# Low halves on VectorE alone, half splits one turn sooner, and RWKV's key factor on VectorE, in a two-block transformer kernel

## The reference

```python
z = u @ w_in[i]
a = jax.nn.sigmoid(a0 + xa @ a2)
kk = heads(k * k_k)
kk = kk / jnp.maximum(jnp.sqrt(jnp.sum(kk * kk, axis=-1, keepdims=True)), 1e-12)
k = k * (1.0 + (a - 1.0) * k_a)
...
h = h + rmsnorm(merged @ w_out[i], mix_post_norm[i])
f = rmsnorm(h, ffn_pre_norm[i])
f = jnp.square(jax.nn.relu(f @ w_ff_in[i])) @ w_ff_out[i]
h = h + rmsnorm(f, ffn_post_norm[i])
e = (p[i] @ w_ple[i]) * jax.nn.sigmoid(h @ w_ple_gate[i])
```

## Time and profile before

| what | us |
|---|---|
| median of 3 runs | 1006.86 (1006.79 to 1007.04) |
| the profiled execution | 1004.86 |
| its span, first to last instruction | 1003.0 |
| TensorE busy | 947.7 |
| VectorE, ScalarE, GpSimd busy | 567.2, 431.0, 222.5 |
| GpSimd: 33 halves, 54 steps of 384 columns, 4 halves of W_ple_gate | 86.6, 82.1, 11.6 |

### The profile page before, as it was taken

The page is one execution under the profiler, slowest core; times in us unless marked ns, Lnnn a source line. Parts: engine busy times, 40 slices in busy tenths (PEclk is TensorE's granted clock), DMA queues, the critical chain, the costliest instruction groups (busy, mean ns, idle before and its releaser), DMA issues.

```text
span 1003.0 us, 15853 instructions
## 1 busy us (share of the span) xinstructions
PE 947.7 (94%) x6780; PEld 776.2 (77%) x6780; DVE 567.2 (57%) x867; ACT 431.0 (43%) x687; POOL 222.5 (22%) x151
## 2 busy tenths in 40 slices
PE   6999999989989999999989999989999999999996
PEld 3988887767558988888769988766568688888875
DVE  1558665653474444677864656864663344444883
ACT  2575234343342334455542433663440345454560
POOL 1000000100000254566630450000000023434570
PEclk9999999999999999999999999999999999999998
DMA  9334333212534865555337673332465367665531
GB/s 335 101 126 143 110 89 125 85 45 85 210 132 160 249 194 181 197 191 187 125 126 169 153 213 116 126 126 85 160 218 147 89 166 198 178 192 186 190 104 42
DMA packets 134949, 151.85 MB, mean 151 GB/s; under 512 B 15936, under 2 KB 106304, under 8 KB 134752
## 3 DMA queue, kind: packets, MB, share of 16 engines
q1 hardware_dynamic: 133952, 147.14, 47.4%
q10 hardware_dynamic: 928, 3.70, 1.0%
HBM read 149.78 MB, written 1.05 MB: 150 GB/s over the span
## 4 chain that ended last, share of the span: by engine, by line
PE 79%; DVE 12%; ACT 5%; issue 2%; DMA 1%; POOL 0%; POOLq 0%; SPq 0%; ACTq 0%; DVEq 0%
PE psum L806 10%; PE psum L695 7%; PE psum L697 7%; PE psum L696 7%; PE psum L758 7%; PE psum L807 6%; PE psum L1292 4%; PE psum L778 3%; PE psum L779 3%; PE psum L787 3%; PE psum L701 2%; PE psum L864 2%; ACT parts L1697 2%; PE psum L854 2%; PE psum L855 2%
## 5 line engine op out<-in xcount | busy, mean ns | idle before, releaser
L1697 ACT ACTIVATE parts<-low 128x1024 fp32r<-128x1024 f32 (+2 forms) x234 | 238.6, 1047 | 110.6 <-PE psum L697 61.9
L695 PE MATMUL psum<-parts 128*128 128x512 f32 (+2 forms) x424 | 171.7, 405 | 11.6 <-DVE parts L2430 8.6
L2430 DVE TENSOR_TENSOR parts<-low,parts 128x1024 fp32r<-128x1024 f32 (+2 forms) x115 | 144.1, 1261 | 55.0 <-ACT parts L1697 54.4
L697 PE MATMUL psum<-parts 128*128 128x512 f32 (+2 forms) x424 | 164.3, 387 | 0.0
L696 PE MATMUL psum<-parts 128*128 128x512 f32 (+2 forms) x424 | 164.0, 387 | 0.0
L806 PE MATMUL psum<-parts 128*128 128x512 f32 x434 | 155.6, 398 | 0.0
L1697 ACT ACTIVATE high<-psum 128x512 f32<-128x512 f32 (+5 forms) x103 | 56.3, 565 | 184.8 <-PE psum L809 73.0
L807 PE MATMUL psum<-parts 128*128 128x256 f32 x496 | 129.1, 281 | 0.0
L3252 POOL TENSOR_TENSOR parts<-low,parts 128x1024 fp32r<-128x1024 f32 x33 | 86.6, 2625 | 118.4 <-ACT parts L1697 118.4
L695 PEld LDWEIGHTS psum<-parts 128*128 128x128 f32 x424 | 80.0, 189 | 34.2 <-DVE parts L2430 7.6
L807 PEld LDWEIGHTS psum<-parts 128*128 128x128 f32 x496 | 93.6, 189 | 5.7
(11 more groups left out here) (304 smaller groups left out, 1493.6 us busy)
## 6 DMA issues: line engine op xcount, KB each, us to landing
low<-in_w_in_dram SPq DMA_DIRECT2D x40, 1024.0 KB, 5.3
low<-in_w_ffn_in_dram SPq DMA_DIRECT2D x44, 512.0 KB, 5.1
low<-in_w_ff_in_dram SPq DMA_DIRECT2D x16, 1024.0 KB, 5.7
low<-in_w_ff_out_dram SPq DMA_DIRECT2D x16, 1024.0 KB, 4.9
low<-in_w_ffn_out_dram SPq DMA_DIRECT2D x11, 1024.0 KB, 4.9
low<-in_w_out_dram SPq DMA_DIRECT2D x8, 1024.0 KB, 5.9
low<-in_w_ple_gate_dram SPq DMA_DIRECT2D x4, 1024.0 KB, 4.9
low<-in_w_up_dram SPq DMA_DIRECT2D x3, 1024.0 KB, 5.0
```

The lines of the kernel that those rows point to most:

```text
L695: mm(o, l[0], r[0], start, False)
L697: return mm(o, l[1], r[0], False, stop)
L1697: return e.activation(o, a, ACT.Copy)
L2430: tt(rslot3(n, nk, width)[:, r, 0:w], slot3(n, nk, width)[:, r, 0:w], st.hi3(j)[:, r, 0:w].bitcast(F32), ALU.subtract) \
```

## The change

It does four things. GpSimd makes no low part any more: VectorE makes half 1 of the slots of `ff` and `fn`, all 1024 columns of a down step, and both halves of `pg`. In all streams half 1 of the next slot is split one turn sooner, on ScalarE and on VectorE. KM is made by VectorE (four TENSOR_SCALAR), A4 by Qi ahead of KM by k. And 1/norm is one power of -0.5 on GpSimd instead of ScalarE's square root and VectorE's reciprocal; ScalarE's table load for it goes, and the one behind it that brought the other table back.

```diff
         def parted(tag, j, first):
-            if first or ST[tag].whole:
-                return split_dve.at(tag, j, 0 if first else 1)
-            return split_pool.at(tag, j)
+            return split_dve.at(tag, j, 0 if first else 1)
...
-                q.wait_ge(*rw_dve.at("ni"))
+                q.wait_ge(*rw_pool.at("ni"))
...
             def feature_chunk(st, j, widths, read):
                 steps = 1 + len(widths)
                 for n in range(steps):
-                    if n in (0, steps - 1):
-                        split(st, j + 1, (1 if n else 0,))
+                    if n < 2:
+                        split(st, j + 1, (n,))
                     yield
...
                     for i in range(2):
-                        split(st, j0 + s + 1, (i,))
-                        for _ in range(nk // 2):
+                        for r in range(nk // 2):
+                            if i == 0 and r < 2:
+                                split(st, j0 + s + 1, (r,))
                             yield
...
-                for c in range(4):
-                    s = slice(256 * c, 256 * c + 256)
-                    act(KM[:, s], A4[:, s], ACT.Identity, scale=vec("rwkv_k_a", c), bias=omka[:, c:c + 1]).then_inc(rw_act.up("km", c), 1)
-                yield
-                q.wait_ge(*rw_dve.at("n"))
-                act(knorm, knorm, ACT.Sqrt).then_inc(rw_act.up("n"), 1)
...
-                for h in [h for h in parts if h == 0 or st.whole]:
+                for h in parts:
...
                 for n in range(1 + len(widths)):
                     yield
-                    if n == 0:
-                        split(st, j + 1, (0,))
-                split(st, j + 1, (1,))
+                    if n < 2:
+                        split(st, j + 1, (n,))
                 read()
...
-                            if r == 1:
+                            if (i, r) in ((0, 1), (1, 0)):
                                 split(st, j0 + s + 1, (i,))
...
-                for h in range(2 if tag != "pg" else 1):
+                for h in range(2):
...
-                tt(rview(OR + 2048 * n + 1024 * (k % 2), 1024)[:, 0:640], slot(n)[:, 1024 * (k % 2):1024 * (k % 2) + 640],
-                   rview(base, 1024)[:, 0:640].bitcast(F32), ALU.subtract).then_inc(down_dve.up(tag, "wl", k), 1)
+                tt(rview(OR + 2048 * n + 1024 * (k % 2), 1024), slot(n)[:, 1024 * (k % 2):1024 * (k % 2) + 1024],
+                   rview(base, 1024).bitcast(F32), ALU.subtract).then_inc(down_dve.up(tag, "wl", k), 1)
...
                 ts(knorm, p[:, 0:16], 1e-24, None, ALU.max, None).then_inc(rw_dve.up("n"), 1)
-                q.wait_ge(*rw_act.at("km", 3))
+                yield
+                q.wait_ge(*rw_act.at("a", 1, 1))
+                for c in range(4):
+                    s = slice(256 * c, 256 * c + 256)
+                    ts(KM[:, s], A4[:, s], vec("rwkv_k_a", c), omka[:, c:c + 1], ALU.mult, ALU.add).then_inc(rw_dve.up("km", c), 1)
+                yield
+                q.wait_ge(*rw_act.at("qi"))
+                q.wait_ge(*rw_dve.at("km", 3))
+                tt(A4, A4, Qi, ALU.mult).then_inc(rw_dve.up("aq"), 1)
+                yield
                 tt(KM, KM, zk_f, ALU.mult).then_inc(rw_dve.up("km"), 1)
-                yield
-                q.wait_ge(*rw_act.at("n"))
-                e.reciprocal(knorm, knorm).then_inc(rw_dve.up("ni"), 1)
-                yield
-                q.wait_ge(*rw_act.at("qi"))
-                tt(A4, A4, Qi, ALU.mult).then_inc(rw_dve.up("aq"), 1)
-                yield
...
-                yield from steps(14)
+                q.wait_ge(*rw_dve.at("n"))
+                tt(knorm, knorm, mh.broadcast_to([128, 16]), ALU.pow).then_inc(rw_pool.up("ni"), 1)
+                yield
+                yield from steps(13)
```

More of the change, by code:

```diff
@@ L478, in __init__ @@
                 self.tag, self.W, self.slots, self.shapes = tag, W, slots, shapes
-                self.whole = tag in ("st1", "st2")
                 self.uh, self.ul, self.hi, self.both = uh, ul, hi, both
@@ L546, in program @@
         z_act, z_dve, z_pool = count("z_act"), count("z_dve"), count("z_pool")
-        split_act, split_dve, split_pool = count("split_act"), count("split_dve"), count("split_pool")
+        split_act, split_dve = count("split_act"), count("split_dve")
         main_pe, main_act, main_dve, main_pool = [count("main_" + n) for n in ("pe", "act", "dve", "pool")]
@@ L552, in program @@
         up_pe, up_dve = count("up_pe"), count("up_dve")
-        wo_pe, wo_act, wo_dve, wo_pool = [count("wo_" + n) for n in ("pe", "act", "dve", "pool")]
-        down_pe, down_act, down_dve, down_pool = [count("down_" + n) for n in ("pe", "act", "dve", "pool")]
+        wo_pe, wo_act, wo_dve = [count("wo_" + n) for n in ("pe", "act", "dve")]
+        down_pe, down_act, down_dve = [count("down_" + n) for n in ("pe", "act", "dve")]
         stick_pe, stick_act, stick_dve = [count("stick_" + n) for n in ("pe", "act", "dve")]
@@ L850, in block @@
                         k, c = 4 * (n // 2) + kk, slice(512 * kk, 512 * kk + 512)
-                        q.wait_ge(*(wo_dve.at(tag, "lo", n, 0) if kk < 2 else wo_dve.at(tag, "lo", n, 1) if tag != "pg" else wo_pool.at(tag, "lo", n)))
+                        q.wait_ge(*wo_dve.at(tag, "lo", n, kk // 2))
                         q.wait_ge(*wo_act.at(tag, "th", i, k // 4))
@@ L882, in down_part @@
                 q.wait_ge(*down_dve.at(tag, "al", k))
-                q.wait_ge(*down_pool.at(tag, "wl", k))
+                q.wait_ge(*down_dve.at(tag, "wl", k))
                 for n in range(2):
@@ L1896, in rwkv @@
                 act(fct, fct, ACT.Exp, scale=-S0).then_inc(rw_act.up("f"), 1)
-                q.wait_ge(*rw_act.at("a", 1, 1))
-                q.wait_ge(*init_dve.at("omka"))
-                for c in range(4):
-                    s = slice(256 * c, 256 * c + 256)
-                    act(KM[:, s], A4[:, s], ACT.Identity, scale=vec("rwkv_k_a", c), bias=omka[:, c:c + 1]).then_inc(rw_act.up("km", c), 1)
                 yield
-                q.wait_ge(*rw_dve.at("n"))
-                act(knorm, knorm, ACT.Sqrt).then_inc(rw_act.up("n"), 1)
                 for _ in range(3):
@@ L3243, in root @@
                 tt(rs, rs, mh, ALU.pow).then_inc(seam_pool.up(tag, i, name), 1)
-            def split(st, j):
-                if j == len(st.slots) or st.whole:
-                    return
-                nk, width, w = st.shape(j)
-                r, n = slice(nk // 2, nk), held(st.tag, j)
-                q.wait_ge(*split_act.at(st.tag, j, 1))
-                tt(rslot3(n, nk, width)[:, r, 0:w], slot3(n, nk, width)[:, r, 0:w], st.hi3(j)[:, r, 0:w].bitcast(F32), ALU.subtract) \
-                    .then_inc(split_pool.up(st.tag, j), 1)
             def head(tag, st, read, late):
@@ L3263, in head @@
                             read(n)
-                            if n == 0:
-                                split(st, 0)
             def feature_chunk(st, j, widths, read, late):
-                split(st, j + 1)
                 late()
@@ L3279, in token_range @@
                 for s in range(n):
-                    split(st, j0 + s + 1)
                     for i in range(2):
@@ L3285, in token_range @@
                             yield
-            def split_wo(tag, n):
-                whole, hi, lo_ = slot(held(tag, n)), rview(WO[tag][1][n], 2048), rview(OR + 2048 * held(tag, n), 2048)
-                q.wait_ge(*wo_act.at(tag, "hi", n, 1))
-                tt(lo_[:, 1024:2048], whole[:, 1024:2048], hi[:, 1024:2048].bitcast(F32), ALU.subtract).then_inc(wo_pool.up(tag, "lo", n), 1)
-            def split_down(tag, k):
-                _, hid, K, o, o_tail = DOWN[tag]
-                base = o + 1280 * (k % 3) if k < K - 8 else o_tail + 1280 * (k - K + 8)
-                n, c = held(tag, k // 2), 1024 * (k % 2)
-                q.wait_ge(*down_act.at(tag, "wh", k))
-                tt(rview(OR + 2048 * n + c, 1024)[:, 640:1024], slot(n)[:, c + 640:c + 1024], rview(base, 1024)[:, 640:1024].bitcast(F32),
-                   ALU.subtract).then_inc(down_pool.up(tag, "wl", k), 1)
             def rope(tag, n, m, zs, t1, cos):
@@ L3407, in gpsimd_program, with ff_in @@
             turns.beside(steps(11), seam("ff", 0, True), 9)
-            def ff_in(tag, down):
+            def ff_in(tag):
                 st = ST[tag]
@@ L3413, in ff_in @@
                 for j in range(len(st.slots)):
-                    if j + 1 == len(st.slots):
-                        for k in range(2):
-                            split_down(down, k)
                     yield from feature_chunk(st, j, [128, 128], nothing, nothing)
-            def down_first(tag):
-                for k in range(2, DOWN[tag][2]):
-                    split_down(tag, k)
             def seam_gate(i):
@@ L3425, in seam_gate @@
                 yield from steps(3)
-            turns.beside(ff_in("ff", "dn1"), seam("ff", 1, True), 4)
```

(9 more changed lines are left out.)

2 lines of the change are left out of this document (1 added, 1 removed).

## The result

The kernel before took 1006.95 us (median of 4 executions, 1006.79 to 1007.27), the changed one 988.8 us (4 executions, 988.69 to 989.79): ratio 0.9822, 95% interval 0.9805 to 0.9839. That is 18.15 us less, where 12.4 were forecast, and only 0.3 us inside the lower end of the range (988.5). The profiled executions are 1004.86 and 988.69 us, their spans 1003.0 and 986.9: 16.1 us less.

What follows compares the result with a forecast made beforehand. TensorE, busy 947.7 of 1003.0 us, was taken as the bound, leaving some 55 us of stops. Terms summed to 12.4 us off, giving 994.5 us against the median of 1006.86; range 988.5 to 1001.5 us with the faster rivals.

Steps and rivals of the forecast that it cites:

- No cost in the feed-forwards: Both feed-forwards: GpSimd's 33 halves, 41 us of work, go to VectorE beside TensorE's products and cost nothing.
- Ends of the down projections: Tails of both down projections: TensorE's four stops behind VectorE's low parts go or shrink, -3.0 us, bounds 0 and -3.6.
- restarts: All places: every stop that goes also saves a restart of 0.1 to 0.15 us, -1.0 us for eight.
- W_ple_gate: Gate's weight behind the first down projection: two stops go, one shrinks, -2.6 us, bounds -1 and -3.2.
- Key factor: RWKV's key: the 3.11 us stop until 77.58 goes, GpSimd's power may cause another, -1.3 us, bounds -0.5 and -3.1.
- 108.52, 253.41, 631.15: TensorE stops in the mixers, at these times in us, go or shrink through sooner halves: -1.3, -0.6 and -1.2 us.
- The clock: Behind the stop at 631.15: with a shorter stop the granted clock stays up, -1.4 us (1.7 at four in five).
- Much is given back: Rival: in the mixers removed stops return at the next chain step, only -5.6 us stays, 1001.5 us; chance 0.15.
- more goes than the list: Rival: no lock at GpSimd's power (-1.8 us more) and shorter small stops of TensorE, 989 us; chance 0.16.

Runs made afterwards that it cites:

- A: The kernel before with only GpSimd's bulk work moved to VectorE, nothing else of the change: 1001.32 us, ratio 0.9939.
- A with B: The kernel before with the whole change but for the sooner turns: 994.57 us, ratio 0.9882.
- B: The kernel before with only the key factor on VectorE and the power of 16 columns on GpSimd: 1002.77 us, ratio 0.9952.
- C: The kernel before with only half 1 split one turn sooner on ScalarE and VectorE, GpSimd as before: 1003.27 us, ratio 0.9971.

## Why the prediction was right, and where it was off

- **No cost in the feed-forwards** (33 halves): right, 15.6 us of VectorE in 25 where 16.4 were worked out.
- **Ends of the down projections, -3.0**: right in the mechanism, 1.22 and 0.42 us a step; mis-sized at -4.2, beyond its bound of -3.6. The term counted the idle time of four stops; each also delays the products right behind it, by 0.3 us on average. The same goes for the **restarts**: 0.1 to 0.15 each was too little, the rows say 0.04 to 0.4 over the idle time.
- **W_ple_gate, -2.6**: right, -3.1. The four halves and the add took 4.7 us where 5.2 were forecast. The forecast left 0.6 us of the stop at 519, and 1.2 is left; what it didn't have was 0.5 at 512.
- **Key factor, -1.3**: the step that failed. It took the whole length of GpSimd's power as time in which VectorE is held, by the row of a half of 1024 columns. With subtractions of 384 columns in its place the stop is 1.5 us, inside the 1.2 to 2.4 that were worked out; with the power of 16 it is none, and the term is -3.3. That the power begins only when VectorE's half is done was right. Rows of before could have told the rest: 384 columns cost 0.82 us and 1024 cost 2.2, both the same for a column. The Trainium skill ("SBUF — State Buffer", section "SBUF: two separate sides") has VectorE and GpSimd exclude each other at their common port pair, for a whole instruction. With the exclusion these runs agree: VectorE's steps wait 0.6 to 2.2 us for GpSimd's subtractions and products, and the power waits for VectorE's half. With the whole instruction the power doesn't agree: VectorE ran its steps of 1.22 us during the 2.75 us that it took.
- **108.52, 253.41, 631.15**: -1.5, -0.75 and -1.3 for -1.3, -0.6 and -1.2. Right at the places, but what went at 631 came back (below).
- **The clock, -1.4**: -1.5 at the place, and that it fits is luck. The run of A alone had the stop at 631 in full and no fall behind it; its fall came 30 us later, behind another stop. And A gave the 1.6 us back within 6 us, so the fall was not worth its length.
- **The rivals.** "Much is given back" was right for the second mixer: 2.7 us of the 2.8 won there by the stop and the clock, where the forecast had 2.6 off. Held against A with B, which has no fall there, the sooner turns take 1.3 and 1.4 us from two stops and lose 2.5 at others. In the first mixer nothing came back, and "more goes than the list" held there: 1.8 us in small stops, and 2.0 at the power. So the 16.1 us are not the forecast's 12.4 with each term a little larger: 2.6 were forecast in the second mixer, which gave 0.1, and the first gave 3.8 more than was forecast.
- **The median.** Of the 18.15 us, 16.1 are in the profiled executions. The other 2 are because before's profiled execution was 2.1 us under its median and after's was at it, and no trace accounts for them; 0.7 more of the 16.1 are a clock that happened to rise sooner at the start. Executions of before range from 1004.4 to 1010.8 at mean granted clocks of 0.987 to 0.995; those of after were all at 0.996. The stop of 3.1 us at 77 had a fall of the clock behind it in the runs of A and of C, so a part of the 2 us is likely such falls in executions without a trace. But some executions of before at 0.995 took 1006.8, and what they spend is open.

## What to carry to other kernels

GpSimd's work beside VectorE's costs each VectorE instruction a wait that grows with GpSimd's columns and not with VectorE's own: taking a third of a step's elements over made the whole step slower, 1.64 us where all of it takes 1.22 alone. So ask how many columns GpSimd works on, not how long it takes. Count a stop as more than its idle row, but before counting the gain from one, look at who is next on the chain that didn't move: here ScalarE's three functions took back what a sooner half had won, until a part of them was moved. A stretch at the low clock can hide a wait in the same way, and then the clock is worth nothing. And a half placed into a gap in which an engine waits anyway beats one placed in front of its chain.

## What the runs showed of the hardware

- GpSimd's two-tensor instructions hold VectorE's two-tensor steps beside them by 0.82 us at 384 columns, 1.10 at 512 and 2.2 at 1024, some 2.1 ns a column, and as much a step of 0.41 us as one of 1.22. In place on one tensor, 384 columns cost 0.63.
- GpSimd's power of 16 columns takes 2.75 us, and before that it waits for a VectorE half that is under way, up to 1.2 us: 2.92 to 3.92 us in the rows. It adds 0.02 us to the VectorE step beside it. Whether a wide power holds VectorE as a wide subtraction does wasn't tried.
- TENSOR_SCALAR with one tensor in SBUF is held as well: 1.38 us for four became 3.09.
- TensorE's clock fell to its 1.2 GHz level for 3.4 us, or 6.8, at or behind stops, but not behind the same ones in each execution: before at 284 and 632, A at 78, 221, 286 and 665, B at 280 and 628, C at 77, 220, 285 and 667, A with B at 656, the changed kernel at 275. The falls of 3.4 us at 78, 221, 656 and 665 cost 1.4 to 1.7 us each; the one at 632 cost nothing, since without it TensorE waits 1.58 us for VectorE. The spread of the executions doesn't show which kernel has fewer falls: the 4 of the changed kernel spread by 1.1 us, the 4 of before beside them by 0.5, and 17 of before on another occasion by 6.4.
